# The last stage of a three-block network on one core: mLSTM, its input projections and the gated attention's output projection in one phase

## The reference, cut to what matters

```
h = rmsnorm(x);  parts = h @ w_in + b_in          # split into hg_*, gla_*, ml_*
y_gla = GLA output, gated and normed (4 heads x 128)
q, k  = silu(causal_conv4(ml_q, ml_k) + conv_b);  q = q / 8        # 4 heads x 64
i, f  = ml_i, log_sigmoid(ml_f)                    # 4 + 4 columns: the gates
b     = cumsum(f) in a chunk; d[t,s] = b[t]-b[s]+i[s] (s <= t)
m[t]  = max(b[t]+m_prev, max_s d[t,s]);  w = exp(d-m);  inter = exp(b+m_prev-m)
s     = (q k^T) * w
num   = inter*(q C) + s v;   den = inter*(q n) + sum(s)
out   = num / max(|den|, exp(-m)) * sigmoid(ml_o)
y_ml  = rmsnorm_per_head(out) * norm_w * silu(ml_z)
x     = x + concat(y_hg, y_gla, y_ml) @ w_out;   result = rmsnorm(x) * final_w
```

## Time and profile before

| | |
|---|---|
| median of three runs | 4503.98 us (4496.69 to 4504.25) |
| the profiled execution: time, span | 4506.79 us, 4505.1 us |
| mean granted TensorE clock | 0.943 |
| PE busy in the span | 90% |
| DVE, ACT, POOL busy | 36%, 19%, 10% |

### The profile page before, as it was taken

How to read it: one execution, slowest core, us unless ns; L and a number is a source line. 1 busy time by engine, 2 the same in 40 slices (tenths; PEclk the granted TensorE clock), 3 DMA queues, 4 the chain that set the end, 5 groups by cost and what they waited for, 6 DMA issues and landing times. The chain is left out here.

```text
span 4505.1 us, 32474 instructions
## 1 busy us (share of the span) xinstructions
PE 4067.3 (90%) x13311; PEld 2093.6 (46%) x13311; DVE 1615.8 (36%) x2312; ACT 862.6 (19%) x969; POOL 428.4 (10%) x496
## 2 busy tenths in 40 slices
PE   6897899999799899977989999999899999798887
PEld 3454343454354677443434444444355555453453
DVE  6475113121323454143232443434445542312433
ACT  2111202100234121244020000000324321300222
POOL 0143000000000232021001222122000000000000
PEclk8998899999989999998989999999999999888998
DMA  3222110211001111110011111111101001012001
GB/s 113 66 68 52 66 38 28 61 33 38 19 22 36 29 38 29 52 33 10 24 33 47 47 47 38 47 47 39 32 19 39 19 19 33 5 45 70 10 8 40
DMA packets 287985, 172.95 MB, mean 38 GB/s; under 512 B 24047, under 2 KB 278878, under 8 KB 287582
## 3 DMA queue, kind: packets, MB, share of 16 engines
q1 hardware_dynamic: 248848, 124.86, 10.0%
q0 software_dynamic: 9856, 23.87, 2.0%
q10 hardware_dynamic: 29134, 22.14, 1.7%
HBM read 157.63 MB, written 13.21 MB: 38 GB/s over the span
## 5 line engine op out<-in xcount | busy, mean ns | idle before, releaser
L161 PE MATMUL products<-normed,weights 128*128 128x512 f32 x1664 | 730.4, 600 | 41.1 <-ACT normed L992 36.3
L161 PEld LDWEIGHTS products<-normed,weights 128*128 128x128 f32 x1664 | 318.8, 193 | 440.8 <-issue 438.7
L161 PE MATMUL products<-gate,weights 128*128 128x512 f32 x896 | 392.6, 600 | 18.8 <-POOLq L3546 7.6
L2552 PE MATMUL products<-normed,weights 128*128 128x512 f32 (+1 forms) x672 | 304.7, 603 | 5.0 <-DVE normed L391 5.0
L161 PE MATMUL products<-residual,weights 128*128 128x512 f32 x672 | 295.4, 598 | 0.9 <-ACT work L1289 0.9
L161 PEld LDWEIGHTS products<-gate,weights 128*128 128x128 f32 x896 | 172.1, 192 | 239.6 <-issue 216.0
L161 PEld LDWEIGHTS products<-residual,weights 128*128 128x128 f32 x672 | 128.7, 192 | 161.9 <-issue 158.1
L2552 PEld LDWEIGHTS products<-normed,weights 128*128 128x128 f32 (+1 forms) x672 | 122.7, 189 | 151.1 <-issue 149.2
L179 PE MATMUL products<-weights,normed 128*128 128x512 f32 x384 | 167.5, 598 | 5.0 <-DVE normed L391 5.0
L1029 DVE TENSOR_TENSOR residual<-products,residual 128x1024 f32<-128x1024 f32 x32 | 39.2, 1224 | 285.6 <-PE products L161 285.6
L278 PE MATMUL products<-gate,s_small 128*128 128x512 f32 x320 | 139.9, 592 | 0.0
(11 more groups left out here) (522 smaller groups left out, 5724.2 us busy)
## 6 DMA issues: line engine op xcount, KB each, us to landing
weights<-in_w_in_dram SPq DMA_DIRECT2D x80, 512.0 KB, 3.8
weights<-in_w_up_dram SPq DMA_DIRECT2D x32, 512.0 KB, 4.2
weights<-in_w_down_dram SPq DMA_DIRECT2D x32, 512.0 KB, 4.4
weights<-in_sgu_w_in_dram SPq DMA_DIRECT2D x24, 512.0 KB, 3.8
weights<-in_s_w_in_dram SPq DMA_DIRECT2D x16, 512.0 KB, 4.0
weights<-in_w_out_dram SPq DMA_DIRECT2D x24, 256.0 KB, 2.8
work<-in_x_dram ACTq DMA_DIRECT2D x8, 512.0 KB, 10.1
branch_scratch<-work POOLq DMA_DIRECT2D x8, 512.0 KB, 2.9
```

The costliest lines, as they stand in the source:

```text
L161: last = pe.matmul(out[0:cols, half * BANK:(half + 1) * BANK], slot(c, b, kt, cols)[:, k, :], acts[n][:, half * BANK:(half + 1) * BANK], s ...
L2552: last = pe.matmul(out[0:cols, half * BANK:(half + 1) * BANK], slot(c, f.b, kt, cols)[:, kk, :], acts[kk][:, half * BANK:(half + 1) * BANK ...
```

## The change

The three barriers behind the GLA branch go: GLA's output projection, the mLSTM input phase, the mLSTM phase and its output projection become one phase. The barrier at the end of `decay_phase` stays. The gate projection becomes the last fill of `decay_phase`, with the 8 gate columns stationary, and its result is copied and turned by 8 small transposes in the new phase. The exponents of all heads have buffers of their own and are made ahead of the heads; the convolutions no longer use padded buffers; sigmoid(o) is applied before the denominator; the head's result is written into `M`, and norm and gate are applied by separate steps. The weight list gets the gate block in `decay_phase`, and dummy blocks up to a multiple of 4 ahead of v.

```
-LOADS = (... ("ml", 3), ("ml_rows", 2))
+LOADS = (... ("ml", 2), ("ml_rows", 2))
 decay_phase:
+    add("ml", U - 1, 0, [(w[:, SEG["ml_i"]:SEG["ml_i"] + 8], KT, 8)], 16)
+    ml_gates = fills.pop()
+        work = columns_product(ml_gates, x, KT, 8)
         for h in range(per(U - 1)):
+            advance(ml_gates.quanta // per(U - 1))
             normalise(U - 1, h)
 its scalar part, after the last head's square:
+                act.activation(c.ml_gates_rows, take_group(c, act, ml_gates.g)[0:8, :], ACT.Copy)
 mlstm_phase:
+    a.E = [tile(12), tile(13), c.C[:, 4, :], c.C[:, 5, :]]
+    order = [("raw", 0), ("raw", 1), ("cums", 0), ("raw", 2), ("rows", 0)]
+    order += [("v", i) for i in range(TT)] + [("gla", m) for m in range(KT)]
+    order += [("qk", 0), ("qk", 1), ("turn", 0), ("raw", 3), ("S", 0), ("N", 0)]
+    order += [("o", 0), ("den", 0), ("num", 0), ("o", 1), ("qk", 2), ("qk", 3), ("turn", 1), ("norm", 0)]
+    order += [("den", 1), ("num", 1), ("z", 0), ("norm", 1), ("S", 1), ("N", 1)]
+    order += [("o", 2), ("den", 2), ("num", 2), ("z", 1), ("norm", 2)]
+    order += [("o", 3), ("den", 3), ("num", 3), ("z", 2), ("norm", 3), ("z", 3)]
+        elif what == "v" and n == 0:
+            while len(c.plan.blocks) % 4:
+                c.plan.add_blocks(columns(c, w, SEG["ml_v"], 1), at)
 tensor:
+        taken(c, pe, c.ml_gates_group)
         for i in range(TT):
-            for k in range(KT):
-                last = pe.matmul(c.pb[:, 1, i * 8:(i + 1) * 8], h[k][:, i * P:(i + 1) * P], gate_w[:, k, :], ...)
+            last = pe.transpose(c.pb[:, 1, i * 8:(i + 1) * 8], c.ml_gates_rows[:, i * P:(i + 1) * P], c.ident[0:8, 0:8])
...
+        for m in range(2):
+            start_group(c, pe, g_out + m)
+            block_ready(c, pe, b_out + m)
+            out_piece(m, 0, 3)          # output projection, heads 0 to 2
+        for m in range(2):
+            out_piece(m, 3, 4).then_inc(c.group_done, 1)
+        for m in range(2, KT):
+            product_ct(c, pe, g_out + m, [(b_out + m, 4, P)], [M[:, kk, :] for kk in range(HEADS)])
 scalar:
+        take(0); take(1); silu(0)
+        act.wait_ge(c.ml_rows, 2)
+        act.dma_start(ml_rows_dram(c), ml.rows).then_inc(c.ml_stored, 16)
+        take(2); silu(1)
+        act.wait_ge(c.ml_stored, 16)
+        act.dma_start(ml.M, src[0].partition_broadcast(P)) ...
+        act.dma_start(ml.floor, src[1].partition_broadcast(P)) ...
+        silu(2)
...
+        for h in range(HEADS):
+            weights(h)                  # the two exponentials of a head
 vector, between the values v0 to v7:
+        value(0); value(1)
+        dve.wait_ge(c.params_loaded, loaded("ml_rows"))
...                                     # running maxima
+        value(2)
...
+        value(3)
         tt(ml.floor, ml.floor, ml.M, ALU.add, c.ml_floor)
+        value(4); exponents(0); value(5); exponents(1); value(6); value(7)
+            if what == "gla": residual add; after the last: exponents(2); exponents(3)
+            elif what == "raw": convolve(n)
 build:
-        then(branch_out_phase(c, t, 512), meet=True)
-        then(mlstm_input_phase(c, t), meet=True)
-        then(mlstm_phase(c, t), meet=True)
         sums = Sums(c)
-        then(branch_out_phase(c, t, 1024, sums))
+        then(mlstm_phase(c, t, sums))
```

More of the change, by code:

```diff
@@ L2917, in decay_phase, with ml_rows_dram @@
     return Phase(loads=loads, tensor=tensor, scalar=scalar, vector=vector)
[L2920 to L2939, removed]
+def ml_rows_dram(c):
+    return c.gates_dram.rearrange("q (n t) -> (q n) t", t=P)[0:64, :]
 def mlstm_memory(c):
     a = c.ml = Core()
[L2945 removed]
+    tile = lambda n: c.W[:, n * SEQ:(n + 1) * SEQ]
+    a.q, a.k = [tile(0), tile(1)], [tile(2), tile(3)]
     a.M = c.W[:, 4096:8192]
     a.floor = c.W[:, 8192:12288]
[L2948 to L2949 removed]
+    a.E = [tile(12), tile(13), c.C[:, 4, :], c.C[:, 5, :]]
+    a.raw = [a.E[0], a.E[1], a.E[0], c.C[:, 7, :]]
+    a.squares = c.C[:, 7, :]
+    small = [c.s5b[:, n * SEQ:(n + 1) * SEQ] for n in range(3)]
+    a.kT, a.den, a.S, a.N = [small[0], c.C[:, 6, :]], small[0], small[1], small[2]
     cols = c.levels[:, :, :].rearrange("p a n -> p (a n)")
@@ L2973, in mlstm_input_phase @@
[L2973 to L2983, removed]
@@ L2987, in loads, with rows, pair @@
+    g_out = c.plan.groups
+    b_out = len(c.plan.blocks)
+    for m in range(KT):
+        c.plan.add_blocks(columns(c, t["w_out_3"][0], P * m, 1, 1024 // P, 4), g_out + m)
+    c.plan.groups += KT
+    def rows(h):
+        return slice((h % 2) * 64, (h % 2 + 1) * 64)
+    def pair(h):
+        return c.pb[:, 2 * (h % 2):2 * (h % 2) + 2, :].rearrange("p a n -> p (a n)")
     def loads(act):
-        act.dma_start(gate_w, w[:, SEG["ml_i"]:SEG["ml_i"] + 8].rearrange("(k p) n -> p k n", p=P)).then_inc(c.params_loaded, 16)
@@ new lines, in out_piece @@
+        def out_piece(m, first, last):
+            out = c.pa[:, ((g_out + m) % 2) * SEQ:((g_out + m) % 2 + 1) * SEQ]
+            for kk in range(first, last):
+                if m == 0:
+                    pe.wait_ge(c.decay_y, norms + kk + 1)
+                for half in range(HALVES):
+                    ins = pe.matmul(out[:, half * BANK:(half + 1) * BANK], slot(c, b_out + m, 4, P)[:, kk, :],
+                                    M[:, kk, half * BANK:(half + 1) * BANK], start=(kk == 0), stop=(kk == HEADS - 1))
+            return ins
@@ new lines, in scalar @@
+        for what, n in order:
+            if (what, n) not in g:
+                continue
+            gg = g[what, n]
+            read = c.group_read[gg % 2]
+            if (what, n) == ("raw", 3):
+                take(3)
+                silu(3)
+            elif what == "o":
+                act.wait_ge(c.ml_carried, n + 1)
+                act.activation(M[:, n, :], take_group(c, act, gg), ACT.Sigmoid, bias=c.v3["ml_o"][:, n:n + 1]).then_inc(read, 1)
+            elif what == "den":
+                if n:
+                    act.wait_ge(c.ml_h, n)
+                act.activation(ml.den, take_group(c, act, gg), ACT.Abs).then_inc(read, 1)
+            elif what == "num":
+                act.wait_ge(c.ml_h, n + 1)
+                act.activation(ml.squares, M[:, n, :], ACT.Square).then_inc(c.decay_squared, 1)
+            elif what == "z":
+                act.wait_ge(c.ml_floor_used, n + 1)
+                act.activation(floor[:, n, :], take_group(c, act, gg), ACT.Silu, bias=c.v3["ml_z"][:, n:n + 1]).then_inc(read, 1)
+            elif what == "norm":
+                inverse_root(c, act, take_group(c, act, gg), D_MODEL / DV).then_inc(read, 1)
```

362 lines of the change are left out of this document (171 added, 191 removed).

## The result

| | before | after |
|---|---|---|
| median | 4504.11 us (4496.69 to 4509.11, 4 runs) | 4398.43 us (4397.41 to 4404.00, 4 runs) |
| span of the profiled execution | 4505.1 us | 4402.2 us |
| mean granted clock | 0.943 | 0.955 |

The ratio is 0.977, with a 95% interval of 0.975 to 0.979: 105.7 us less. The forecast was 4401, the range 4387 to 4422.

The account below looks back on a forecast made before the run. TensorE, busy 90%, bounds it; time comes from its waits, low clock or fewer matmuls. 3935.0 + 417.3 + 3.3 + 5.3 + 3.3 = 4364.2 against 4467.25, 103 us less: median 4401, range 4387 to 4422.

Parts of the forecast that it names:

- The gap of 25.6: TensorE's wait after qk and turn for broadcast rows, maxima and exponents; claimed to go whole, 25.6 us.
- the 9.3: The same wait for the second pair of heads; claimed to go too, 9.3 us.
- the 14.3: Four waits of a norm for ACT's squares, 14.3 us; claimed to go since o1, den, num or z stand between.
- The decay phase's end: Gate fills beside two norms waiting for squares: 13.7 us of matmuls for 0.7, barrier ending at about 3935.0.
- Start of the phase: Behind the remaining barrier: eight transposes 2.0 us, then 3.3 lost while the clock rises in the first products.
- The rows: Broadcast rows, stored after raw 2, reach DVE at about 4001; 5 us of slack before v4 needs v2 read.
- Matmuls: All TensorE work of the new phase at full clock, with the 8 transposes: 417.3 us.
- New waits: Waits the new order brings at o0, S1, N1, o2, o3 and z3: together 5.3 us, bounds 0 and 15.
- 8.9 against the 7.6 of S and N: Before o0: DVE's wait, convolution and state take 8.9 us, S and N cover 7.6; with latencies a 1.5 us wait.
- Falls of the clock: In the new phase: one fall taken at 3.3 us, a fall costing 3.3 to 5; bounds 0 and 15.
- Weight loads: Three dummy blocks loaded ahead of v; nothing waits at 3.8 us a load.
- rival 1: New phase: four or five clock falls instead of one, 3 to 4 times 4 us, 4413 to 4417; chance 0.12.

Follow-up runs that it names:

- Number 8: Changed kernel with the old order inside a head (o, den, num, z, norm) and ScalarE's square behind z's silu: 4426.20 us.
- number 2: Changed kernel with the gate projection taken out of the decay phase's end and put first in the merged phase: 4410.61 us.
- number 5: Changed kernel with the exponents of heads 2 and 3 put behind VectorE's wait for turn 1: 4416.41 us.
- number 4: Changed kernel with the exponents of heads 2 and 3 made just ahead of the wait for turn 1, not behind GLA's last add: 4403.39 us.
- Number 1: Kernel before with only the gate projection changed: last fill of the decay phase, 8 columns stationary, turned by 8 transposes; barriers kept: 4469.59 us.
- number 7: Changed kernel with each head's z one place earlier and exponents of heads 2 and 3 behind VectorE's wait for turn 1: 4408.75 us.
- number 3: Changed kernel with the old 64 gate matmuls (8 moving columns) between raw 0 and raw 1, no gate fill in the decay phase: 4420.90 us.
- number 9: Changed kernel with a barrier of all engines put back behind GLA's last add, ahead of the first qk: 4405.10 us.

## Why the prediction was right, point by point

- **What bounds it:** right. The stage gave back its waits and its low clock. The gap of 25.6 went whole, the 9.3 and the 14.3 too. Number 8 shows that the order alone carries the 14.3, and not the barriers.
- **The decay phase's end:** forecast 25.0 us from the last common fill's end to the barrier's, measured 25.4. That the cover is real, number 2 shows.
- **Start of the phase:** the small matmuls with the transposes 2.5 us, measured 1.4 (the transposes 0.95); the climb 3.3, measured 2.1 (29.6 us for 32 instructions of 0.858).
- **The rows:** forecast at VectorE at about 4001, measured 3998.7. Raw 2 ended at 3983.1, where I had put it, and the store, the loads and the small steps ahead of them took 15.5 us of the 18 that I gave them. From the read of v2 to the start of v4 lie 6.0 us, where I counted 5.
- **Matmuls:** den and num 13.23, as forecast. S and N took 6.07 and 6.66 us against 7.6 each, qk 3.43 against 4.05: rows at mixed clock, taken too literally. Together 3.7 too much. Against that, some 1.6 remain that no single term shows; a norm ahead of a wait takes 1.88 for the 1.72 that I gave it, o 1 13.93 up to the next matmul for 13.73.
- **New waits:** 5.3 forecast, 7.9 measured, all at named places except for their sizes: o 0 2.96 (1.5), N 1 1.46 (0.3), o 2 1.00 (1.4), S 1, o 3 and z 3 0.83 each (0.7). For o 0, the step "8.9 against the 7.6 of S and N" failed in its second half: S and N at full clock take 6.07, so they hide less. So the same mistake made the term of S and N 1.5 too dear and this wait 1.5 too cheap, and in the sum it cancelled.
- **Falls of the clock:** one forecast at 3.3, one came, in o 0, at 1.7 (15.70 us against the 14.00 of a projection at full clock). That it was one is in part luck: in number 2 the same wait brought none.
- **Weight loads:** none was waited for, as forecast; no wait for one stands in the list above.
- **Sum:** the stage was to shrink by 103.05 us and shrank by 106.0. That is closer than its terms: the start of the phase, the matmuls and the fall came out 7.6 us cheaper, the decay phase's end and the waits 3.0 dearer, and 1.6 are in no term. The span came out at 4402 as forecast only since the stage began 3.05 us late, which is no effect of the change.
- **The bound that was wrong:** "a fall costs 3.3 to 5 (in den and num, if as long)". In number 5 it cost 11.8. Had the order put a gap of that size before a den, the forecast would have missed by more than its rival 1 allowed for (4 each). The change has one new wait above 1.5 us, and it stands before a projection.
- **Early exponents:** the forecast gave them the 9.3. That is right for their place ahead of the waits (number 5: 18.4), but number 4 shows that VectorE has room for the second pair just before turn 1 as well. Making them as early as the change does isn't what pays.

The rule of the Trainium skill that I weighed ("TensorE: Matmul & The Clock Gate", Part 4: PE-mode transpose: transposes don't count as busy) isn't settled, but one pair of runs speaks against it. Number 1 and the kernel after issue the same up to the barrier and wait the same 7.63 us there. Behind it number 1 starts GLA's projection at once (3933.55), the kernel after first its 1 us of transposes (3938.41). In both the clock rose just over 5 us after that start, and not 1 us later with the transposes:

```profile
3938.55:3939.05 0.50, 0.50 (x2) 0.19 (x1) 0.00 (x0) 0.00 (x0) 0.00 (x0) 0.91 0.00 0
3943.41:3943.91 0.50, 0.50 (x2) 0.19 (x1) 0.00 (x0) 0.50 (x1) 0.00 (x0) 0.94 0.00 0
```

The first line is of number 1, the second of the kernel after; the 0.5 us ahead of each stand at 0.50. The 3.3 of the kernel before belong to a rise some 6 us after the start, behind norms that had waited and run at low clock.

## What to carry to other kernels

Price a gap of TensorE as the gap plus the low clock of what is issued behind it, and put the coarse projections behind the unavoidable gaps, not a chain like den and num. Other fine matmuls have to be looked at one by one: S came back to full clock within some 4 us, den and num not in 23. An operation in a strictly ordered queue costs nothing anywhere ahead of a wait that is longer than it, and its full length just behind it: read the idle time before the queue's waits first. Compare a stage between two marks in the trace: the code ahead of it, though the same, ended up to 12 us earlier or later from execution to execution.

## What the runs showed of the hardware

- **Behind the same gap, two ways back.** After 6.51 us without work den and num ran 23.15 us at 0.50, TensorE busy throughout; after 6.52 us a projection was at 1.00 in the second 4 us (numbers 5 and 7). The Trainium skill ("TensorE: Matmul & The Clock Gate", Part 1: The HAM clock gate) calls the way back a matter of time and not of the number of matmuls. The projection fits that; den and num don't, and there the measurement decides.
- **The clock can fall without a gap.** With 8 moving columns it went from 0.93 to 0.50 at 100% busy (number 3). But den and num started at 1.00 stay there (number 7). Den and num kept whichever level they began at; why is open.
- **128 moving columns alone don't hold the clock down.** S of the first pair in the kernel before multiplies with 128 moving columns as well (64 stationary), starts behind the 25.6 us gap, and is at 1.00 some 4 us on; its second pair, behind 9.2 us, too. So the number of moving columns doesn't explain den and num. The rows of the first pair:

```profile
4179.50:4181.50 2.00, 2.00 (x10) 2.00 (x11) 1.97 (x3) 0.00 (x0) 0.00 (x0) 0.50 0.00 0
4181.50:4183.50 2.00, 2.00 (x18) 2.00 (x17) 1.97 (x3) 0.00 (x0) 0.00 (x0) 0.69 0.00 0
4183.50:4185.50 2.00, 2.00 (x28) 2.00 (x27) 1.73 (x5) 0.00 (x0) 0.00 (x0) 1.00 0.00 0
```

- **A fall isn't certain.** The wait of 2.96 or 2.97 us before o 0 gave an o 0 of 15.70 in most kernels, but in number 2 it was 14.00 with the clock at 1.00. A barrier's 1.36 us gave a fall in number 9, where the clock was still 1.00 over the first 2 us of qk, and none in number 1. I can't say what decides it.
- **8 stationary columns cost what 128 cost:** 16 records of 8 columns in 6.96 us (3921.84 to 3928.80), where a projection of 128 columns has 32 in 14.00 and the earlier trace rows have 32 of 16 columns in 14.4.
